# One scatter an item in place of four, and one TensorE loop over all items, in a mixture-of-experts block

## The reference

```
logits = (xt @ w_router + b_router)
top_val, top_idx = lax.top_k(logits, 4)
top_w = softmax(top_val)
# for each expert e, over the rows of xt that are sent to it (blocks of 128 rows)
gate = minimum(xblk @ w_gate[e] + b_gate[e], 7)
up   = clip(xblk @ w_up[e] + b_up[e], -7, 7)
h    = (up + 1) * gate * sigmoid(1.702 * gate)
yb   = h @ w_down[e] + b_down[e]
y    = segment_sum(yb * row_w[:, None], row_tok)
```

## Time and profile before

| | us |
|---|---|
| median of 3 runs (2564.26 to 2574.02) | 2564.54 |
| the profiled execution's own time | 2564.66 |
| its span | 2562.8 |
| TensorE matmuls busy | 2263.5 (88%) |
| VectorE busy | 857.8 (33%) |
| GpSimd busy | 642.9 (25%) |
| ScalarE busy | 531.3 (21%) |

### The profile page before, as it was taken

How to read it: one execution, slowest core, us unless ns; L and a number is a source line. 1 busy time by engine, 2 the same in 40 slices (tenths; PEclk the granted TensorE clock), 3 DMA queues, 4 the chain that set the end, 5 groups by cost and what they waited for, 6 DMA issues and landing times.

```text
span 2562.8 us, 54558 instructions
## 1 busy us (share of the span) xinstructions
PE 2263.5 (88%) x21771; PEld 1083.6 (42%) x21772; DVE 857.8 (33%) x1261; ACT 531.3 (21%) x1209; POOL 642.9 (25%) x631
## 2 busy tenths in 40 slices
PE   5999999998987699999989979799889898999960
PEld 3575756775552234443433433233333333334320
DVE  4155465363452222321322323123212323132213
ACT  5122213222442111111211111111111111111111
POOL 5000000000133132323233333333333323232342
PEclk9999999999986899999999989899999899999985
DMA  8112110135034677596899897899777797999954
GB/s 270 33 33 74 34 58 17 58 110 214 33 140 133 234 277 283 164 340 224 307 390 373 304 364 261 314 327 338 249 246 268 272 381 244 347 373 365 397 176 143
DMA packets 227008, 587.48 MB, mean 229 GB/s; under 512 B 26506, under 2 KB 98306, under 8 KB 226786
## 3 DMA queue, kind: packets, MB, share of 16 engines
q1 hardware_dynamic: 133794, 338.47, 35.0%
q10 hardware_dynamic: 55504, 197.22, 19.6%
q0 software_dynamic: 37648, 50.92, 9.7%
HBM read 548.73 MB, written 37.78 MB: 229 GB/s over the span
## 4 chain that ended last, share of the span: by engine, by line
PE 41%; DMA 39%; issue 9%; DVE 6%; POOLq 2%; ACT 2%; POOL 1%; ACTq 0%; DVEq 0%; SPq 0%
DMA y_rows<-yrow,idx_s 31%; PE ps L1673 10%; DMA xg<-xn_rows,idx_g 7%; PE ps L1459 5%; PE ps L1703 5%; PE ps L1455 4%; PE ps L1560 4%; PE ps L1465 2%; PE ps L1516 2%; PE ps L1462 2%; DVE xr L1339 2%; POOLq L426 1%; PE ps L1611 1%; PE ps L1538 1%; PE ps L1431 1%
## 5 line engine op out<-in xcount | busy, mean ns | idle before, releaser
L1673 PE MATMUL ps<-w_gu_e,xT 128*32 128x512 f32 x9216 | 1013.7, 599 | 58.0 <-DMA w_gu_e<-in_w_up_dram 31.2
L1703 PE MATMUL ps<-w_down_e,hT 128*32 128x256 f32 x9216 | 529.8, 391 | 111.9 <-issue 75.7
L1673 PEld LDWEIGHTS ps<-w_gu_e,xT 128*32 128x32 f32 x9216 | 300.6, 111 | 745.7 <-issue 698.6
L658 POOL DMA_INDIRECT y_rows<-yrow,idx_s x188 | 324.8, 1728 | 642.0 <-DMA y_rows<-yrow,idx_s 581.0
L1703 PEld LDWEIGHTS ps<-w_down_e,hT 128*32 128x32 f32 x9216 | 305.2, 113 | 350.9 <-issue 169.1
L1316 DVE STREAM_TRANSPOSE gu_t<-ps 128x1024 f32<-128x1024 f32 x94 | 111.9, 1228 | 498.2 <-PE ps L1673 497.4
L907 ACT ACTIVATE xT<-xr,fm 128x128 f32<-128x128 f32 x384 | 153.0, 481 | 515.3 <-PE ps L1673 508.2
L923 ACT ACTIVATE yrow<-ps,slot_tab 128x256 f32<-128x256 f32 x188 | 73.8, 475 | 810.6 <-DMA y_rows<-yrow,idx_s 724.6
L1339 DVE STREAM_TRANSPOSE xr<-xg 128x1024 f32<-128x1024 f32 x49 | 60.9, 1244 | 527.9 <-DMA xg<-xn_rows,idx_g 527.9
L645 POOL DMA_INDIRECT xg<-xn_rows,idx_g x196 | 219.9, 1122 | 61.7 <-issue 58.5
L609 POOL DMA_INDIRECT slot_rows<-slot_row,slot_at x32 | 31.3, 980 | 686.9 <-DVE slot_row L1226 679.2
(11 more groups left out here) (275 smaller groups left out, 1469.8 us busy)
## 6 DMA issues: line engine op xcount, KB each, us to landing
w_down_e<-in_w_down_dram ACTq DMA_DIRECT2D x368, 512.0 KB
w_gu_e<-in_w_gate_dram SPq DMA_DIRECT2D x256, 512.0 KB
w_gu_e<-in_w_up_dram SPq DMA_DIRECT2D x256, 512.0 KB
w_ring<-in_w_ada_dram SPq DMA_DIRECT2D x17, 1024.0 KB, 5.2
w_ring<-in_w_in_dram SPq DMA_DIRECT2D x20, 512.0 KB, 5.2
w_first<-in_w_ada_dram SPq DMA_DIRECT2D x7, 1024.0 KB, 12.4
x_all<-in_x_dram SPq DMA_DIRECT2D x2, 2048.0 KB, 10.5
w_out<-in_w_out_dram SPq DMA_DIRECT2D x8, 512.0 KB, 8.5
```

Of the source, the lines that this page charges most:

```text
L658: G.indirect_dma_start(y_quarters, bass.IndirectOffsetOnAxis(ap=idx_s[:, g:g + 1].bitcast(U32), axis=0), yrow[:, g, :], None, compute_op=A ...
L1673: last = T.matmul(ps[j * GROUP:(j + 1) * GROUP, g, :].rearrange("p (w b f) -> p w b f", w=2, f=GROUP), xT[:, k, g * GROUP:(g + 1) * GROUP] ...
L1703: last = T.matmul(ps[j * GROUP:(j + 1) * GROUP, 4 + g // 2, g % 2 * QUARTER:(g % 2 + 1) * QUARTER], hT[:, g, k, :], w_dn[:, k, j * QUARTER ...
```

## The change

The weighted rows are written so that each token's row stands whole in one partition: for group g and quarter j an activation takes the 32 partitions of quarter j and writes them to the 32 partitions of group g, at quarter j of the row. These are sixteen activations of 32x256 an item in place of four of 128x256. One scatter then moves 128 rows of 4 KB. Its index is one column of a table (row_tab) that VectorE makes once. Since all groups' empty slots are now in one scatter, there are 128 spare rows in place of 32. In POOL's loop the four gathers of item i+4 are issued first, then the scatter of item i.

TensorE's code outside the loop is gone. The loop has two rounds more than there are items; round n is down of item n-2 and then gate_up of item n, and the size of a part that doesn't exist is 0 (a size is now 0 to 4, before it was coded as 0 to 3). Semaphore counts are shifted by starting increments so that the waits of the empty parts are met.

```diff
-        hT, yrow = r("hT", GROUPS, KT, GROUP), r("yrow", GROUPS, QUARTER)
+        hT, yrow = r("hT", GROUPS, KT, GROUP), r("yrow", D)
...
-            pool.dma_start(y_dram[SEQ:SEQ + GROUP, :], box[0][0:GROUP, 0:D]).then_inc(y_added, 16)
+            pool.dma_start(y_dram[SEQ:SEQ + BLOCK, :], box[0][:, 0:D]).then_inc(y_added, 16)
...
-            def scatter_begun(m):
-                pool.wait_ge(yr_ready, m + 1)
-                apart(pool)
-                slots_of(m, idx_s, sidx_made)
-
-            def scatter(m, g):
-                pool.wait_ge(y_added, m * (16 * GROUPS) + 16 * (Y_ZERO + g))
-                apart(pool)
-                G.indirect_dma_start(y_quarters, bass.IndirectOffsetOnAxis(ap=idx_s[:, g:g + 1].bitcast(U32), axis=0),
-                                     yrow[:, g, :], None, compute_op=ALU.add).then_inc(y_added, 16)
+            def scatter(m):
+                col = item_column(pool, m)
+                pool.wait_ge(y_added, m * 16 + 16 * Y_ZERO)
+                apart(pool)
+                G.tensor_copy(idx_s[:], row_tab[:, bass.ds(col >> 2, 1)]).then_inc(sidx_made, 1)
+                pool.wait_ge(sidx_made, m + 1)
+                pool.wait_ge(yr_ready, m + 3)
+                apart(pool)
+                G.indirect_dma_start(y_dram, bass.IndirectOffsetOnAxis(ap=idx_s[:].bitcast(U32), axis=0), yrow[:],
+                                     None, compute_op=ALU.add).then_inc(y_added, 16)
...
             with pool.Fori(0, n_before) as i:
                 gather_begun(i + 4)
-                scatter_begun(i)
                 for g in range(GROUPS):
-                    scatter(i, g)
                     gather(g)
+                scatter(i)
...
                 act.wait_ge(d_used, m * KT + KT)
-                act.wait_ge(y_added, m * (16 * GROUPS) + 16 * Y_ZERO)
+                act.wait_ge(y_added, m * 16 + 16 * Y_ZERO)
                 apart(act)
                 for g in range(GROUPS):
-                    last = A.activation(yrow[:, g, :], ps[:, 4 + g // 2, g % 2 * QUARTER:(g % 2 + 1) * QUARTER],
...
+                    for j in range(4):
+                        js = slice(j * GROUP, (j + 1) * GROUP)
+                        last = A.activation(yrow[g * GROUP:(g + 1) * GROUP, j * QUARTER:(j + 1) * QUARTER],
...
-            gate_up(0, 32, size)
-            e, size = item_expert(pe, 1), item_size(pe, 1)
-            gate_up(1, e * 32 + 32, size)
-
-            with pe.Fori(0, n_before) as i:
-                pair = item_pair(pe, i)
-                down(i, pair & 3)
-                gate_up(i + 2, (pair >> 4) * 32, (pair >> 2) & 3)
-            down(n_before, item_size(pe, n_before))
-            down(n_last, item_size(pe, n_last))
+            with pe.Fori(0, n_rounds) as n:
+                pair = item_pair(pe, n)
+                down(n, (pair >> 3) & 7)
+                gate_up(n, (pair >> 6) * 32, pair & 7)
```

More of the change, by code:

```diff
@@ L418, in item_expert, with rounds @@
             return eng.value_load(int_e[0:1, bass.ds(m, 1)], min_val=0, max_val=NE - 1)
-        def item_size(eng, m):
-            return eng.value_load(int_v[0:1, bass.ds(m, 1)], min_val=0, max_val=GROUPS - 1)
+        def rounds(eng):
+            return eng.value_load(int_n[0:1, 2:3], min_val=NE + 2, max_val=ITEMS + 2)
         def item_column(eng, m):
@@ L428, in item_pair @@
         def item_pair(eng, m):
[L430 removed]
+            return eng.value_load(int_q[0:1, bass.ds(m, 1)], min_val=0, max_val=64 * NE + 63)
         def last_item_of(eng, e):
@@ L668, in _ @@
                 gather_begun(i + 4)
-                scatter_begun(i)
                 for g in range(GROUPS):
-                    scatter(i, g)
                     gather(g)
[L673 to L676, removed]
+                scatter(i)
+            scatter(n_before)
+            scatter(n_last)
             pool.wait_ge(xg_in, n_last * (16 * GROUPS) + 3 * 16 * GROUPS)
@@ L930, in _ @@
             n_last = last_item(act)
+            act.sem_inc(yr_ready, 2)
             rows_scaled(0)
@@ L1343, in _ @@
             rows_turned(1)
+            dve.wait_ge(slots_in, 16 * 4)
+            for g in range(GROUPS):
+                gs = slice(g * GROUP, (g + 1) * GROUP)
+                last = V.tensor_scalar(row_tab[gs, :], slot_tab[gs, g:NCOL:GROUPS, 0], 0.25, spare[gs, 0:1], ALU.mult,
+                                       ALU.add)
+            last.then_inc(row_tab_made, 1)
             rows_begun(dve, range(len(y0_sb)))
+            dve.sem_inc(hT_ready, 1)
             swiglu(0, link)
@@ L1653, in gate_up @@
                 pe.wait_ge(xT_ready, m + 1)
-                if not (isinstance(m, int) and m < 1):
-                    pe.wait_ge(gu_evac, m * 2)
+                pe.wait_ge(gu_evac, m * 2)
                 apart(pe)
-                with pe.If(size > 1):
-                    with pe.If(size == 3):
+                with pe.If(size > 2):
+                    with pe.If(size == 4):
                         gate_up_of(loaded, (2, 3), False)
@@ L1661, in gate_up @@
                         gate_up_of(loaded, (2,), False)
-                with pe.If(size > 0):
+                with pe.If(size > 1):
                     gate_up_of(loaded, (0, 1), True)
                 with pe.Else():
-                    gate_up_of(loaded, (0,), True)
+                    with pe.If(size > 0):
+                        gate_up_of(loaded, (0,), True)
+                    apart(pe)
             def gate_up_of(loaded, groups, ends):
@@ L1679, in gate_up_of, with down, down_of @@
                         last.then_inc(gu_used, 1)
-            def down(m, size):
-                pe.wait_ge(hT_ready, m + 1)
-                if not (isinstance(m, int) and m < 1):
-                    pe.wait_ge(yr_ready, m)
+            def down(n, size):
+                pe.wait_ge(hT_ready, n)
+                pe.wait_ge(yr_ready, n)
                 apart(pe)
-                with pe.If(size > 1):
-                    with pe.If(size == 3):
-                        down_of(m, (2, 3), False)
-                    with pe.Else():
-                        down_of(m, (2,), False)
-                with pe.If(size > 0):
-                    down_of(m, (0, 1), True)
+                with pe.If(size > 2):
+                    with pe.If(size == 4):
+                        down_of(n, (2, 3), False)
+                    with pe.Else():
+                        down_of(n, (2,), False)
+                with pe.If(size > 1):
+                    down_of(n, (0, 1), True)
                 with pe.Else():
-                    down_of(m, (0,), True)
-            def down_of(m, groups, ends):
+                    with pe.If(size > 0):
+                        down_of(n, (0,), True)
+                    apart(pe)
+            def down_of(n, groups, ends):
                 for k in range(KT):
-                    pe.wait_ge(dn_in[k], m * 16 + 16)
+                    pe.wait_ge(dn_in[k], n * 16)
                     for g in groups:
```

66 lines of the change are left out of this document (38 added, 28 removed).

## The result

The changed kernel took **2499.69 us** (2495.58 to 2502.65, four runs) beside 2566.33 us (2564.26 to 2574.02) for the kernel before: a ratio of **0.9734, interval 0.9708 to 0.9759**. The forecast was 2462, its range 2425 to 2515. Direction and stated range hold, but the forecast's own inner range, 2440 to 2485, does not, and some 37 us of the gain are missing. The same kernel was measured twice more during the experiments, word for word the same, and took **2468.36 us** (2464.10 to 2472.71; ratio 0.9611, interval 0.9585 to 0.9637) and **2465.99 us** (2459.80 to 2467.65; ratio 0.9623, interval 0.9602 to 0.9644). Both repeats lie inside the inner range. So there are two things to read: what the change did, and what cost 31 us more in the first measurement.

The account below looks back on a forecast made before the run. Bound: the serial scatter and yrow-write chain, about 38 us an item, exposed at short items, with the weight stream near its limit. 45.6 + 37 + 27 − 2 − 4 − 1 = 103 off 2564.5 gave 2462 us, range 2425 to 2515.

Parts of the forecast that it names:

- Loop, 1760 to 2440, 45.6: Loop from 1760 to 2440: all down-product waits and low-clock time come back, 34.0 + 11.6 = 45.6 us.
- 1490 to 1760, 37: Loop from 1490 to 1760: 37 of 49.4 us come back, the rest still waiting for down weights after single two-group items.
- the weight stream takes the place of the scatter: Rival, loop: scatter pauses return as weight waits; 2503 us if half of 82.6 returns, 2535 if nearly all; chance 0.16.
- Contention, 4: Weight loads: TensorE without pauses asks sooner, raising the DMA engines' share from 0.88 to 0.93; 4 us charged.
- Tail, 27: After the request of the last down weights: yrow and the last scatter finish earlier, a gain of 27 us.
- Head, −2: TensorE's start: the new loop's jumps delay the first gate/up 16 us, two gaps vanish, 5 back; net 2 us lost.
- One landing, 9 us: Scatter: one of 512 KB replaces four of 128 KB and lands in 9 us, bounds 3.6 to 29.
- POOL's order: POOL's loop: gathers of item i+4 issued before scatter(i), about 5 us while ScalarE writes 6.3; nothing lost.
- Sixteen writes: ScalarE's yrow writes: 6.3 us an item, 4.7 more, covered by gate/up except some tenths at one-group items and the tail.
- slower by landing: Rival, scatter: one lands later than four did, 35 us, exposed items pay 5 us each; 2615 us, chance 0.04.
- The better one: Rival, weight stream: larger rows free 30 us of engine time, gate/up weight waits shrink, jumps won too; 2430 us, chance 0.15.
- Slower by jumps: Rival, TensorE's loop: rounds with a one-group or empty part take two jumps of 4.9 us; 2532 us, chance 0.02.

Follow-up runs that it names:

- pe_only: The kernel before with only TensorE's one loop, its tables and shifted counts; four scatters an item stay: 2562.94 us, ratio 0.9971.
- scatter_only: The kernel before with the rest of the change, one scatter an item, but TensorE's old sequence kept: 2471.76 us, ratio 0.9624.

## Why the prediction was right and wrong

The mechanism was right: the chain of landing, write of yrow, next scatter was what short items waited for, and it is gone. Undisturbed, the change is worth 96 us by the profiled runs (2564.66 − 2468.7) where the sum said 102.6. That the two are so near is partly luck: three terms came out 34 us worse than forecast, the others 27 us better. The terms, read between the same points of both kernels (second measurement for the changed one). Down products of before, then of after, that bound the stretches:
```profile
924.85 3.63 PE L1703 MATMUL ps<-w_down_e,hT 128*32 128x256 f32 x64
...
1489.59 7.09 PE L1703 MATMUL ps<-w_down_e,hT 128*32 128x256 f32 x128
...
1777.97 7.08 PE L1703 MATMUL ps<-w_down_e,hT 128*32 128x256 f32 x128
...
2422.89 13.17 PE L1703 MATMUL ps<-w_down_e,hT 128*32 128x256 f32 x192 [5.15 <-issue]
```
```profile
918.52 3.64 PE L1719 MATMUL ps<-w_down_e,hT 128*32 128x256 f32 x64
...
1473.91 7.09 PE L1719 MATMUL ps<-w_down_e,hT 128*32 128x256 f32 x128
...
1741.60 7.09 PE L1719 MATMUL ps<-w_down_e,hT 128*32 128x256 f32 x128
...
2332.58 3.21 PE L1719 MATMUL ps<-w_down_e,hT 128*32 128x256 f32 x56
```

| stretch (begins at, before / after) | before | after | won | forecast |
|---|---|---|---|---|
| start | 924.85 | 918.52 | 6.3 | −2 (head) |
| 924.85 / 918.52 | 564.7 | 555.4 | 9.4 | 0 |
| 1489.59 / 1473.91 | 288.4 | 267.7 | 20.7 | 37 |
| 1777.97 / 1741.60 | 644.9 | 591.0 | 53.9 | 45.6 |
| 2422.89 / 2332.58, to the request of the last down weights | 39.7 | 56.2 | −16.4 | −4 (contention, wherever) |
| 2462.60 / 2388.73, to SP's read of y | 64.3 | 42.6 | 21.6 | 27 |
| 2526.86 / 2431.36, to the end | 35.9 | 35.5 | 0.4 | −1 |

- *Loop, 1760 to 2440, 45.6*: right in kind, small by 8. The waits for w_gu shrank as well, which I had put at nothing: from 11.4 to 4.4 us in the stretch from 924.85 and from 19.8 to 6.1 in this one.
- *1490 to 1760, 37*: the mis-sized term, 20.7 measured. The down weights came later than an even share says: in the first of the three products the last of them is in 28.5 us after the request (1479.94 to 1508.43), where the sum had 25.4. That product, changed kernel, second measurement:
```profile
1494.55 3.64 PE L1719 MATMUL ps<-w_down_e,hT 128*32 128x256 f32 x64
1498.40 1.07 PE L1719 MATMUL ps<-w_down_e,hT 128*32 128x256 f32 x16 [0.22 <-DMA w_down_e<-in_w_down_dram]
1502.52 1.16 PE L1719 MATMUL ps<-w_down_e,hT 128*32 128x256 f32 x16 [3.05 <-DMA w_down_e<-in_w_down_dram]
1505.87 1.93 PE L1719 MATMUL ps<-w_down_e,hT 128*32 128x256 f32 x16 [2.19 <-DMA w_down_e<-in_w_down_dram]
1508.43 8.82 PE L1719 MATMUL ps<-w_down_e,hT 128*32 128x256 f32 x144 [0.63 <-DMA w_down_e<-in_w_down_dram]
```
  The 13.71 us in front of the product became 6.09 inside it, and TensorE ran at the lower clock around them (granted 0.93 from 1478 to 1528). That is the rival *the weight stream takes the place of the scatter*, in part.
- *Contention, 4*: 16.4 at one place, ahead of the last items, where a down product and the last gate/up product wait for weights. Changed kernel, second measurement:
```profile
2358.97 1.94 PE L1688 MATMUL ps<-w_gu_e,xT 128*32 128x512 f32 x8 [4.58 <-DMA w_gu_e<-in_w_up_dram]
...
2365.88 17.00 PE L1688 MATMUL ps<-w_gu_e,xT 128*32 128x512 f32 x136 [4.97 <-DMA w_gu_e<-in_w_up_dram]
```
  Two loads meet there, and the DMA engines are full (share 1.03 and 385 GB/s from 2332 to 2366). The mean was forecast well: over the stretch of the same items, 1236 to 2346, the share is 0.93 (0.88 before). What it costs was not, since a mean doesn't tell where two loads meet. With the 16.3 us missing from the term before, some 29 of the 82.6 us that were to come back in the loop went to the weight stream.
- *Tail, 27*: 21.6. The steps behind the request of the last down weights, measured and in the sum: write of yrow done after 13.6 us (11.2), the last down product 13.7 more (11.2), the second write 8.0 (7.0), issue and landing 7.3 (7.5). The product waits for yrow and not for weights, and then runs its full 12.8 us.
- *Head, −2*: the other way. The new loop moved the first gate/up from 807.03 to 814.22, 7 us and not 16 (815.78 in `pe_only`, 807.87 in `scatter_only`), and the two gaps of the earlier trace rows went as foreseen. The traces show code arriving there: in the second measurement the instruction queue brings a packet of 16 KB every 3 to 4 us from 801 to 818 and then nearly none, where the kernel before was still fetching at 879. The three comparisons put the new loop at 6 (`pe_only`), 3 to 6 (within the noise) and 12 us won.
- *One landing, 9 us*: 6.3; hidden, so nothing follows. *POOL's order*: free, as forecast.
- *Sixteen writes*: "free, but for some tenths" failed. They take 0.477 us each and not 0.39: the forecast divided the 1.57 us of four wide ones, and a narrow one starts only when the one before has ended, where four wide ones overlap (475 ns each). Their price, 22 to 24 us, stands mostly at the tail and the head, inside terms that I had otherwise.

What no step had is the 31 us of the first measurement; that 2499.69 still lies in the stated range is owed to the width given to the rival of the weight stream. The place of the loss is shown (the stream of weight loads, mostly while a scatter is issued), its cause isn't. The time was long in all four runs of one measurement, whose one profile has the pauses; none of the twelve profiles after it has them, two of them of the same program, on two different chips. Whether how the program was loaded, the chip or a neighbour made it stays open; the place of the code alone is excluded, since unaltered code ran without. Every comparison of the first batch with 2500 us was led astray by it.

Of the rivals, slower by landing is excluded (6.3 us). The better one had the waits for w_gu shrink: they are 30.1 us in the second measurement and 23.8 in the third, against 31.2, though the software queue's share fell from 14.2% to 12.7%; most of what the loop won of them was lost at its end. Slower by jumps is excluded too. From 800 to 2530 the instruction queues moved, in each of the first two measurements of the changed kernel,
```profile
q8 instruction: 6, 0.10, 0.0%
q14 instruction: 5, 0.04, 0.0%
```
and of these nothing between 834 and 2420 us, while TensorE's loop jumped over its bodies in every round. So of the 70 us that the rule on taken branches gave as a rival (the Trainium skill, Runtime: NRT & Kernel Launch, Instruction fetch mechanics) nothing is seen. A one-group gate/up of the changed kernel, second measurement:
```profile
1222.30 7.07 PE L1688 MATMUL ps<-w_gu_e,xT 128*32 128x512 f32 x64
1223.78 7.63 ACT L921 ACTIVATE yrow<-ps,slot_tab 32x256 f32<-32x256 f32 x16 [5.13 <-issue]
...
1232.12 2.15 PE L1719 MATMUL ps<-w_down_e,hT 128*32 128x256 f32 x36 [2.75 <-issue]
```
The gap is 2.75 and not 4.9 us, and it is ScalarE's: its writes end at 1231.41, and the down product begins 0.7 us later. This is also the case that the prediction named as its own end, "if ScalarE's write costs more than 0.5 us each": at 0.477 it is reached already. One slip changes nothing: the shares that the prediction names for its range add up to 0.86 and not 0.83.

## What to carry to other kernels

A chain of small accumulating transfers that wait for each other is priced by its waits, and here one transfer with larger rows replaced it at the landing time of one. When a rearrangement puts many narrow instructions where few wide ones stood, look at the two ends of the loop, where nothing covers them, and share them with an idle engine. When a time differs from the forecast and no wait in the profile accounts for it, measure the unaltered program again before building variants; and check that a variant with the expected total has the expected profile too.

## What the runs showed of the hardware

- One program can run 1.3% slower in all executions of one measurement, at a granted clock of 0.955 against 0.953. Its profile has 75 pauses of 0.62 to 1.12 us between weight loads, 53 of them beside the issue of a scatter; the repeats have 4 and 1.
- TensorE's loop of 49 rounds, with branches over its bodies, loaded no code after its first rounds: no instruction packet between 834 and 2420 us.
- ScalarE's 32x256 writes from PSUM to SBUF, to other partitions, took 466 ns each and did not overlap (7.63 us for sixteen); 128x256 ones took 475 and did (1.57 us for four). On VectorE eight of 32x256 took 3.96 us.
- An accumulating scatter of 128 rows of 4 KB landed in 6.3 and 6.5 us (medians of two measurements), one of 128 rows of 1 KB in 7.3 in the kernel before.
- 256 idle instructions run once ahead of TensorE's loop moved its start by 34.0 us (0.13 each), 64 of them by 3.9.
